# The opening of a hybrid diffusion step in another order, and one layer norm's sums and fillers rearranged

## The reference

```python
def rms_norm(x, g):
    y = xf * lax.rsqrt(jnp.mean(xf * xf, axis=-1, keepdims=True) + EPS)
    return (y * g).astype(x.dtype)

def layer_norm(x, g, b):
    mu = jnp.mean(xf, axis=-1, keepdims=True)
    var = jnp.mean(jnp.square(xf - mu), axis=-1, keepdims=True)
    return (xf - mu) * lax.rsqrt(var + EPS) * g + b

def modulation(cond, w_mod, b_mod):
    m = jax.nn.silu(cond) @ w_mod + b_mod
    return jnp.split(m[..., None, :], 6, axis=-1)

# block 0: h feeds the compression of queries and of keys with values
h = rms_norm(x, norm_mix[0]) * (1.0 + sc1) + sh1
kv = h @ w_dkv ; cq = h @ w_dq
# block 1: between the depthwise convolution and the second pointwise product
y = jax.nn.silu(layer_norm(y, ln_g, ln_b)) ; y @ w_pw2
```

## Time and profile before

| | |
|---|---|
| three runs | 1634.05 us median (1632.44 to 1634.27) |
| the profiled execution | 1635.48 us, of which the span from first to last instruction 1633.7 us |
| PE busy | 1599.7 us, 98% of the span |
| DVE, ACT, POOL busy | 922.9, 666.2, 287.6 us |
| mean granted TensorE clock | 0.995 of full speed |

### The profile page before, as it was taken

How to read it: one execution, slowest core, us unless ns; L and a number is a source line. 1 busy time by engine, 2 the same in 40 slices (tenths; PEclk the granted TensorE clock), 3 DMA queues, 4 the chain that set the end, 5 groups by cost and what they waited for, 6 DMA issues and landing times.

```text
span 1633.7 us, 26252 instructions
## 1 busy us (share of the span) xinstructions
PE 1599.7 (98%) x11123; PEld 1553.6 (95%) x11123; DVE 922.9 (56%) x1541; ACT 666.2 (41%) x1000; POOL 287.6 (18%) x344
## 2 busy tenths in 40 slices
PE   7999999999999999999999999989999999999998
PEld 5889889899999999999999999979999999999998
DVE  5556766766766544554367989987742323223232
ACT  3445545553544423432245656674532212211122
POOL 0011111000165524452342122330000000000000
PEclk9999999999999999999999999999999999999999
DMA  9322332132354434433333298873132122222211
GB/s 321 100 79 85 106 99 78 35 117 78 98 168 139 152 117 138 142 127 123 118 121 98 62 192 162 181 143 101 65 98 76 61 77 78 78 78 72 77 59 65
DMA packets 142381, 178.12 MB, mean 109 GB/s; under 512 B 12945, under 2 KB 121177, under 8 KB 141240
## 3 DMA queue, kind: packets, MB, share of 16 engines
q1 hardware_dynamic: 120048, 109.68, 21.2%
q0 software_dynamic: 21888, 66.66, 16.4%
q10 hardware_dynamic: 328, 0.10, 0.0%
HBM read 148.93 MB, written 2.79 MB: 93 GB/s over the span
## 4 chain that ended last, share of the span: by engine, by line
PE 83%; DVE 9%; DMA 4%; ACT 2%; issue 1%; SPq 1%; POOL 0%; DVEq 0%; ACTq 0%; POOLq 0%
PE PS L699 26%; PE PS L701 25%; PE PS L704 25%; DVE YACC L2350 4%; DMA ZACC<-ZTAP 2%; PE PS L769 1%; PE PS L1041 1%; PE PS L796 1%; PE PS L1052 1%; DMA MODS<-in_w_mod 1%; DMA Y<-SHIFT 1%; PE PS L1004 1%; DVE GP L2314 0%; DVE HL L1930 0%; PE PS L985 0%
## 5 line engine op out<-in xcount | busy, mean ns | idle before, releaser
L699 PE MATMUL PS<-HH,WH 128*128 128x320 f32 x1776 | 410.7, 313 | 8.2 <-DVE HL L1930 7.7
L701 PE MATMUL PS<-HL,WH 128*128 128x320 f32 x1776 | 405.0, 309 | 0.0
L704 PE MATMUL PS<-HH,WL 128*128 128x320 f32 x1776 | 403.8, 309 | 0.0
L1775 DVE TENSOR_TENSOR WL<-RAW,WH 128x2048 fp32r<-128x2048 f32 (+2 forms) x87 | 196.4, 2257 | 203.2 <-ACT WH L1313 203.1
L699 PEld LDWEIGHTS PS<-HH,WH 128*128 128x128 f32 x1776 | 296.0, 188 | 10.2 <-issue 7.2
L701 PEld LDWEIGHTS PS<-HL,WH 128*128 128x128 f32 x1776 | 298.4, 188 | 0.0
L704 PEld LDWEIGHTS PS<-HH,WL 128*128 128x128 f32 x1776 | 298.2, 189 | 0.0
L1313 ACT ACTIVATE WH<-RAW 128x2048 fp32r<-128x2048 f32 (+2 forms) x95 | 171.5, 1805 | 111.3 <-PE PS L704 111.3
L1946 DVE SCALAR_TENSOR_TENSOR X<-PS,MODV,X 128x128 f32<-128x128 f32 (+2 forms) x192 | 72.4, 433 | 198.8 <-PE PS L704 198.7
L621 POOL TENSOR_TENSOR BGACC<-BGACC,BGW 128x512 f32<-128x512 f32 x98 | 135.0, 1378 | 194.9 <-ACT BGW L1569 193.8
L699 PE MATMUL PS<-HIDH,WH 128*128 128x320 f32 x704 | 162.2, 311 | 0.7 <-DVE HIDL L2273 0.7
(11 more groups left out here) (329 smaller groups left out, 2268.4 us busy)
## 6 DMA issues: line engine op xcount, KB each, us to landing
BGW<-in_w_mod POOLq DMA_DIRECT2D x112, 256.0 KB, 3.0
RAW<-in_ffn_w_gate SPq DMA_DIRECT2D x22, 1024.0 KB, 5.3
RAW<-in_ffn_w_up SPq DMA_DIRECT2D x22, 1024.0 KB, 5.3
RAW<-in_ffn_w_down SPq DMA_DIRECT2D x16, 1024.0 KB, 5.1
MODA<-in_w_mod POOLq DMA_DIRECT2D x48, 256.0 KB, 3.8
RAW<-in_conv_w_pw SPq DMA_DIRECT2D x16, 512.0 KB, 5.2
WL<-RAW POOLq DMA_DIRECT2D x8, 1024.0 KB, 9.8
RAW<-in_ffn_w_down SPq DMA_DIRECT2D x8, 768.0 KB, 4.4
```

Source lines behind the costliest of these rows:

```text
L699: mm(o, wh, xh, start=first, stop=False)
L701: mm(o, wh, xl, start=False, stop=False)
L704: ins = mm(o, wl, xh, start=False, stop=last)
L1775: V.tensor_tensor(WL[:, u % 2, 0:n], RAW[:, u % 2, 0:n], WH[:, u % 2, 0:n].bitcast(F32), ALU.subtract).then_inc(lo_done, 1)
```

## The change

In the opening, PE runs the spread of the root ahead of the last quarter of `first_rows`, ACT copies RSTD before MROW, PE runs 14 fillers behind `turn_first`, DVE makes the low part of tile 0 before it scales tile 1, and scales tiles two at a time in the second half. `later_rows(1)` and the two `turn_later` stand a tile or more earlier on PE and between other tiles' work on ACT. The matrices of `MODS[1]` lie in other buffer regions, which no tile of HH or HL uses. In the layer norm, tiles 6 and 7 are summed before tiles 4 and 5, each tile has its own wait, and eight fillers stand ahead of the spread where there were twelve.

```diff
 def tile_order():
-    o += [("stat", "mix0"), ("turn", "mix0"), ("mrow", 0), ("rb", "mix0"), ("mods", 0), ("mrow", 1), ("mods", 1)]
+    o += [("stat", "mix0"), ("turn", "mix0"), ("rb", "mix0"), ("mrow", 0), ("mods", 0), ("mrow", 1), ("mods", 1)]
...
-                   [R_HH + HALF_H, R_HH + HALF_H + 4096, R_HL + HALF_H, R_HL + HALF_H + 4096]
-                   + [R_HID + 32768 + 4096 * i for i in range(4)]]
+                   [R_HID + 20480 + 4096 * i for i in range(7)] + [R_P + 6144]]
...
             def first_rows():
-                rows = begin(("mrow", 0))
                 for k in range(0, KT, 2):
+                    if k == KT - 2:
+                        spread(("rb", "mix0"), diagn, DIAGS["mix0"])
+                    if k == 0:
+                        rows = begin(("mrow", 0))
...
             def second_half(k, j):
                 if (k, j) == (0, 1):
                     later_rows(0)
-                if (k, j) == (3, 1):
+                if (k, j) == (1, 1):
+                    turn_later(0)
+                if (k, j) == (2, 1):
                     later_rows(1)
+                if (k, j) == (3, 0):
+                    turn_later(1)
...
             first_rows()
-            spread(("rb", "mix0"), diagn, DIAGS["mix0"])
-            turn_first()
+            hold_clock(turn_first(), HOLD + 2)
...
             def first_wait(k):
-                if k == KT // 2 - 1:
-                    turn_later(0)
                 if k == KT // 2:
-                    turn_later(1)
                     unit_begin(("dkv", 0))
...
             def square_sums(k):
-                if k < KT - 2:
-                    pe.wait_ge(sem("sq_made"), SQ_BASE["ln"] + k + 3)
-                else:
-                    pe.wait_ge(sem("sq_made"), SQ_BASE["ln"] + KT - 1)
-                    pe.wait_ge(sem("last_squared"), 1)
                 for g in range(GROUPS):
+                    m = k + g // 2
+                    if m < KT - 2:
+                        pe.wait_ge(sem("sq_made"), SQ_BASE["ln"] + m + 2)
+                    elif m == KT - 1:
+                        pe.wait_ge(sem("last_squared"), 1)
...
-            square_sums(4)
-            square_sums(KT - 2).then_inc(mm_done, 1)
+            square_sums(KT - 2)
+            square_sums(KT - 4).then_inc(mm_done, 1)
...
-            hold_clock(rows, HOLD)
+            hold_clock(rows, HOLD - 4)
             spread(("rb", "ln"), diagn, DIAGS["ln"])
...
# ACT
+            spread_copy(("rb", "mix0"), RSTD, QT)
             filled(act, ("mrow", 0))
             A(MROW[:], tile2(("mrow", 0))[:, 0, :], ACT.Copy).then_inc(free_of(("mrow", 0)), 1)
-            spread_copy(("rb", "mix0"), RSTD, QT)
...
-                if k == 2:
+                if k == 3:
                     act.wait_ge(sem("part_rows"), 1)
...
-                if k == 3:
+                if k == 5:
                     filled(act, ("mrow", 1))
...
# DVE, the opening: scale_tile and low_tile are the bodies of the loop of apply()
+            scale_tile("mix0", 0, 0, 0)
+            low_first()
+            low_tile(0, 0, 0, 0)
+            scale_tile("mix0", 0, 0, 1)
+            scale_tile("mix0", 0, 0, 2)
+            low_tile(0, 0, 1, 1)
+            scale_tile("mix0", 0, 0, 3)
+            low_tile(0, 0, 2, 1)
+            low_tile(0, 0, 3, 0)
...
+            first_part(("mods", 1), 0, 4, 6)
+            scale_tile("mix0", 0, 0, 4)
+            scale_tile("mix0", 0, 0, 5)
+            low_tile(0, 0, 4, 1)
+            low_tile(0, 0, 5, 0)
+            filled(dve, ("mods", 1))
+            first_part(("mods", 1), 1, 6, 8)
```

More of the change, by code:

```diff
@@ L881, in turn_first @@
                 turn_rows_of(ps, 0, range(4)).then_inc(mm_done, 1)
+                return ps
             def turn_later(q):
@@ L1249, in square_sums @@
             def square_sums(k):
[L1251 to L1258 removed]
+                for g in range(GROUPS):
+                    m = k + g // 2
[3 more added lines that the diff above has]
+                        pe.wait_ge(sem("last_squared"), 1)
+                    ins = mm(rows[COLG * g:COLG * (g + 1), 0, 0:3 * P], ONES[:, 0:COLG], LNQ[m][:, halves3[g % 2]],
+                             start=(k == 0), stop=(k == KT - 4))
                 return ins
@@ L1904, in scaled_first @@
                 V.tensor_tensor(dst[:], src[:], RSTD[:], ALU.mult).then_inc(sem("first_scaled"), 1)
-            def apply(norm_name, l, half, midway=None, second=None, first=None):
-                was_read(dve, ("rb", norm_name))
-                def scale(k):
-                    if k >= 3:
-                        dve.wait_ge(sem("h_ready"), KT * APPLY[norm_name] + k - 2)
-                    for a, b, s in SEGS:
-                        ins = V.scalar_tensor_tensor(out=SCALED[k % 3][:, a:b], in0=X[:, k, a:b], scalar=GAIN[:, l, half, s, k:k + 1],
-                                                     in1=RSTD[:, a:b], op0=ALU.mult, op1=ALU.mult)
-                    ins.then_inc(sem("t_ready"), 1)
-                    n_t[0] += 1
-                scale(0)
-                if first is not None:
-                    first()
-                for k in range(KT):
-                    ahead = k + 1 < KT and not (second is not None and k + 1 == KT // 2)
-                    if ahead:
-                        scale(k + 1)
-                    n_part[0] += 1
-                    dve.wait_ge(sem("t_ready"), n_t[0] - ahead)
-                    dve.wait_ge(sem("part_hi"), n_part[0])
-                    for a, b, s in SEGS:
-                        ins = V.scalar_tensor_tensor(out=HL[:, k, a:b], in0=SCALED[k % 3][:, a:b],
-                                                     scalar=MODV[:, l, s, 24 * half + k:24 * half + k + 1],
-                                                     in1=HH[:, k, a:b].bitcast(F32), op0=ALU.add, op1=ALU.subtract)
-                    ins.then_inc(sem("h_ready"), 1)
-                    if second is not None:
-                        second(k)
-                        if k + 1 == KT // 2:
-                            scale(k + 1)
@@ new lines, in scale_tile @@
+            def scale_tile(norm_name, l, half, k):
+                if k >= 3:
+                    dve.wait_ge(sem("h_ready"), KT * APPLY[norm_name] + k - 2)
+                for a, b, s in SEGS:
+                    ins = V.scalar_tensor_tensor(out=SCALED[k % 3][:, a:b], in0=X[:, k, a:b], scalar=GAIN[:, l, half, s, k:k + 1],
+                                                 in1=RSTD[:, a:b], op0=ALU.mult, op1=ALU.mult)
+                ins.then_inc(sem("t_ready"), 1)
+                n_t[0] += 1
@@ new lines, in low_tile @@
+            def low_tile(l, half, k, ahead):
+                n_part[0] += 1
+                dve.wait_ge(sem("t_ready"), n_t[0] - ahead)
+                dve.wait_ge(sem("part_hi"), n_part[0])
+                for a, b, s in SEGS:
+                    ins = V.scalar_tensor_tensor(out=HL[:, k, a:b], in0=SCALED[k % 3][:, a:b],
+                                                 scalar=MODV[:, l, s, 24 * half + k:24 * half + k + 1],
+                                                 in1=HH[:, k, a:b].bitcast(F32), op0=ALU.add, op1=ALU.subtract)
+                ins.then_inc(sem("h_ready"), 1)
@@ L1938, in apply @@
+            def apply(norm_name, l, half, midway=None):
+                was_read(dve, ("rb", norm_name))
+                scale_tile(norm_name, l, half, 0)
+                for k in range(KT):
+                    if k + 1 < KT:
+                        scale_tile(norm_name, l, half, k + 1)
+                    low_tile(l, half, k, k + 1 < KT)
                     if midway is not None and k == MIDWAY:
@@ L1997, in late_tile @@
                 V.tensor_copy(KPRAW[:, CTX:CTX + PAST], ps[:, 1, KVL:KVL + P]).then_inc(free_of("late"), 1)
-            def between(k):
-                if k == KT // 2 - 1:
-                    dve.wait_ge(hi_done, 1)
-                    split_first(1)
-                    dve.wait_ge(sem("part_turned"), 1)
-                    first_part(("mods", 1), 0, 4, 6)
-                if k == KT // 2:
-                    filled(dve, ("mods", 1))
-                    first_part(("mods", 1), 1, 6, 8)
             filled(dve, ("mods", 0))
             first_part(("mods", 0), 0, 0, 4)
-            apply("mix0", 0, 0, second=between, first=low_first)
+            was_read(dve, ("rb", "mix0"))
+            scale_tile("mix0", 0, 0, 0)
[7 more added lines that the diff above has]
+            low_tile(0, 0, 3, 0)
+            dve.wait_ge(hi_done, 1)
+            split_first(1)
+            dve.wait_ge(sem("part_turned"), 1)
+            first_part(("mods", 1), 0, 4, 6)
[5 more added lines that the diff above has]
+            first_part(("mods", 1), 1, 6, 8)
+            scale_tile("mix0", 0, 0, 6)
+            scale_tile("mix0", 0, 0, 7)
+            low_tile(0, 0, 6, 1)
+            low_tile(0, 0, 7, 0)
             split_units(U[("dq", 0)])
```

3 lines of the change are left out of this document (removed).

## The result

The changed kernel took 1627.38 us in the median of five runs (1623.79 to 1627.81), the kernel before 1634.05 (1632.29 to 1635.64, five runs beside them): ratio 0.995, with an interval of 0.9938 to 0.9962. That is 6.67 us, where the prediction had 6.6. The five runs are of two kinds: 1623.79 and 1624.62 at a mean granted clock of 0.999, and 1627.38, 1627.70 and 1627.81 at 0.996. The profiled execution is that of 1624.62, so it is one of the short ones, and its span of 1622.8 us is 10.9 shorter than the 1633.7 of before, not 6.7. The extra has to be explained too.

What follows compares the result with a forecast made beforehand. PE was taken as the bound (chain ending last for 83% of the span, busy for 98%). Opening 5.0 + layer norm 1.6 = 6.6 us, so 1634.05 − 6.6 = 1627.4 us, range 1626.0 to 1628.6.

Steps and rivals of the forecast that it cites:

- Start of the first product: Opening: earlier turn of the rows and tile 0's low part made directly start PE's first product 1.26 us earlier.
- Fillers: Opening: 14 fillers, hidden under DVE's work, keep full clock for tile 0, which gains 1.6 us.
- Waits in the first pair: Opening, tiles 0 to 7: the new order removes most of PE's 2.43 us of waits, a gain of 2.1 us.
- The wait of 0.15: Opening: PE's last turn still waits 0.15 us for ACT's last row copy.
- the charge for one more change between kinds of work: Opening, first pair: one more change of work on PE costs about as much as the 0.15 us wait.
- The matrices: Opening: transfers for both later_rows land before PE wants them, with 0.3 us of slack at worst.
- Rival 2: Opening: matrices of later_rows come late and PE waits 1 to 2 us at either part, 1628.9 us; chance 7%.
- Opening in all: Opening: 1.26 + 1.6 + 2.1 = 5.0 us gained.
- Layer norm: Layer norm: new order of sums gains 0.67 us and four fewer fillers 0.9 us, together 1.6 us.
- Rival 3: Layer norm gives 0.7, not 1.6 us, as POOL's transfers of corrected Y tiles come late: 1628.3 us; chance 8%.
- The sum: Whole kernel: 5.0 us from the opening and 1.6 from the layer norm, 6.6 us gained.
- The median: Whole kernel: 6.6 us taken from the median 1634.05, not the profiled 1635.48, since half-clock stretches differ between runs: 1627.4 us.

Runs made afterwards that it cites:

- the opening alone: The changed kernel's opening with the layer norm as in the kernel before: 1628.94 us, ratio 0.9967 to the kernel before.
- the experiment with the clock held: The changed kernel plus three or four fillers at PE's waits in the attention's first and last heads: 1624.90 us, ratio 0.9945 to the kernel before.
- the norm alone: The changed kernel's layer norm with the opening as in the kernel before: 1633.53 us, ratio 0.9999 to the kernel before.

## Why the prediction was right, step by step

- **Start of the first product.** Said: turn at 24.3, MODV 25.3, low part 28.0, product 29.15, a gain of 1.26. Measured: 24.31, 25.37, 28.08, 29.24, a gain of 1.17. Of this 0.43 is the earlier turn (0.35 by the spread's place, 0.08 by an earlier start of the last matrices) and 0.74 the way from the turn to the product, 5.67 us before and 4.93 now, where 0.83 was said. With the spread at its old place that way was 4.86, so the new order on DVE makes it shorter without the spread's new place. The prediction did not see that the spread's old place was itself open to half clock, 1.6 us in two traces; in the trace that it read, the clock was full there.
- **Fillers.** Said: hidden, full clock, 1.6 us. Measured: hidden to 0.01 us and 1.56 us over tile 0 in the trace, 1.32 by `late_rows`. Their removal costs 1629.19 − 1627.38 = 1.8 us in whole times by the medians and 3.3 by the means, a difference that the two kinds of runs leave unsure. They took 3.37 us, not 3.2 to 3.3, with 0.67 to spare. Of the eleven traces that have them one had half clock in them.
- **Waits in the first pair.** Said: 2.43 us of waits, of which 0.15 comes back, and 2.1 gained. Measured: no idle time in PE's rows up to 48.72. From the first product to `late_rows` it was 54.22 − 30.41 = 23.81 us and is 19.48: 4.33 less, of which tile 0 is 1.56, so 2.77 for this step. The step was under-sized by 0.7. The wait of 0.15 did come (0.21 beside the weight load of the last turn). The gain came out larger through the rest: each `later_rows` holds tile 1 and 3 up for 1.87 us from start to start, not 2.0, four and a half tiles behind the last turn take 8.09 us, 1.80 each and not 1.85, and the charge for one more change between kinds of work did not show. The prediction's two workings also disagree: the order that it follows tile by tile ends at 46.9 + 1.85 = 48.75, where 48.72 was measured, while its sum of waits ends at 49.2. Of this step 1.2 us hang on the place of ACT's copies, as the experiment with them shows; the rest, PE's own order and DVE's, was not split further.
- **The matrices.** They were there: the second `later_rows` ran at 37.20, where 37.1 was said, without a wait. Rival 2 did not come.
- **Opening in all.** Said 5.0, measured 5.50 in the trace, and 5.4 in the time of the opening alone.
- **Layer norm.** Said 0.67 + 0.9 = 1.6. Measured 1.47 in the trace: fillers 0.89, sums 0.58; over all traces the sums give 0.28 to 0.68. The prediction let all twelve other rows go into an idle time of 1.17 us. It read that from a trace in which a transfer of Y was late; where none was, the idle time in the old order is 0.58, and two tiles' rows still run when ACT's last square ends. In the two traces of the new order with a late transfer the sums give the 0.67 to 0.68 that was said. In whole times the norm gives 1.0 ± 0.55, so this step may be smaller than the traces say. Rival 3, late tiles of Y, was not seen: the first product is 4.25 us behind RSTD's copy in the kernel after (1089.09 − 1084.84) as with the old norm (1090.02 − 1085.76 = 4.26), and the stretch behind it is equal. POOL's six issues of OFFSET took 5.28 us before and 5.29 after, so nothing stretched them.
- **The sum.** By the traces the two parts are 5.50 + 1.47 = 6.97 us, where 6.6 was said: the first pair 0.7 more, the rest 0.3 less.
- **The median.** Said: the difference is to be taken from the median, since half-clock stretches differ from run to run. That holds, and the experiment with the clock held shows where most of them are. It also shows that 1627.38 came out so near 1627.4 by some luck: three of five runs were of the longer kind. Had two of the five been of the longer kind, not three, the median would have been 1624.62 or near it, below the range.

## What to carry to other kernels

Where TensorE waits it can lose the clock as well as the time, and cheap work that ends before its next input is there kept the clock in ten of eleven traces here; past that point nearly every microsecond of it is paid. Before adding such work, see whether needed work can go into the wait, as the spread did. When one engine's copy waits for another engine's result, look at what is queued behind it: here a copy of 0.38 us held 1.2 us of PE's time only by its place. A wait read from one trace may be that trace's own, as the 1.17 us in the norm were. And where a kernel's runs lie several microseconds apart, first find what they differ in and hold it still, since a step of one microsecond can't be read from times before that.

## What the runs showed that was not expected

- Two stretches in the attention, near 118 and 340 us, run at 1.2 GHz in some executions of the same code and at 2.4 in others, 1.7 us each. In the kernel before PE idled 0.68, 0.89 and 0.88 us ahead of the first one; the changed kernel idled 0.68, 1.00 and 0.78 in its profiled run and kept 1.00. Ten fillers in head 0 and three at each of the last head's last turns ended it.
- Fillers can start at half clock and be slow themselves (4.86 us for 28 rows instead of 3.37), at the price of 0.7 us at the first product, while the tiles behind them ran at full clock.
- Of the transfers Y<-SHIFT one landed some 2 us late in the trace of before, in that without the opening's fillers and in that of the norm alone (ACT waited 3.01, 2.93 and 2.51 us for it, elsewhere about 1). The stretch from SHIFT's copy to the last square, 14.2 us in most traces, was 15.64, 15.81 and 15.15 there. These are just the three traces with a half-clock stretch in the attention, of fourteen. What delays the transfer was not tried.
- Between `late_rows` and SHIFT's copy, 1015 us with the same instructions, traces with no half-clock stretch in the attention differ by up to 1.1 us (1014.99 to 1016.10). That bounds what one pair of traces can say of a step of this size.
